# A two-layer hybrid decoder step on one core: old retention state in two loads, branch A's gate product taken apart, squares summed in column groups, output stored in pieces

## The reference, cut to what matters

```python
def _layer(x, pos, s_wkv, s_ret, s_shift, p):
    h = _rmsnorm(x, p['norm_mix_pre'])
    z = h @ p['w_in']
    ya, s_wkv, s_shift = _rwkv7_branch(za, s_wkv, s_shift, ...)     # branch A
    yb, s_ret = _retention_branch(zb, pos, s_ret, ...)              # branch B
    m = jax.nn.sigmoid(ga) * (ya @ p['w_out_a']) + jax.nn.sigmoid(gb) * (yb @ p['w_out_b'])
    x = x + _rmsnorm(m @ p['w_o'], p['norm_mix_post'])
    h = _rmsnorm(x, p['norm_ffn_pre'])
    f = (jax.nn.silu(h @ p['w_ffn_gate']) * (h @ p['w_ffn_up'])) @ p['w_ffn_down']
    x = x + _rmsnorm(f, p['norm_ffn_post'])

# end of branch A: y = (yn * gain + bias + bonus) * g, with yn = (y - mean) / sqrt(var + eps)
# in branch B, for the samples' old state S0:
    scores = jnp.einsum('bihd,bjhd->bhij', qc, kc) * d_in[None]
    cross = jnp.einsum('bihd,bhde->bihe', qc, S) * d_q[None, :, :, None]
```

## Time and profile before

| | us |
|---|---|
| median of 3 runs | 1365.44 (1364.4 to 1366.78) |
| the profiled execution, its own time | 1364.33 |
| span of its trace | 1362.5 |
| TensorE matmuls busy | 1306.5 (96%) |
| TensorE weight loads busy | 1231.8 (90%) |
| VectorE busy | 865.7 (64%) |
| ScalarE busy | 531.8 (39%) |
| GpSimd busy | 14.7 (1%) |

### The profile page before, as it was taken

The page is one execution under the profiler, slowest core; times in us unless marked ns, Lnnn a source line. Parts: engine busy times, 40 slices in busy tenths (PEclk is TensorE's granted clock), DMA queues, the critical chain, the costliest instruction groups (busy, mean ns, idle before and its releaser), DMA issues.

```text
span 1362.5 us, 27246 instructions
## 1 busy us (share of the span) xinstructions
PE 1306.5 (96%) x11896; PEld 1231.8 (90%) x11896; DVE 865.7 (64%) x1446; ACT 531.8 (39%) x803; POOL 14.7 (1%) x26
## 2 busy tenths in 40 slices
PE   6999999799998999999899999998999989999997
PEld 5899997789997999999888999977999979999996
DVE  4777757666776556653476876667666755656533
ACT  4552032344435333343446521232544354333433
POOL 0002000000000000000000020000000000000000
PEclk8999999899998999999989999998999989999999
DMA  5433223444443454544423322244444534444441
GB/s 201 139 111 126 53 94 118 158 148 152 145 142 124 155 154 153 155 143 151 150 72 115 129 83 71 76 170 156 141 139 132 170 109 125 152 154 142 155 153 56
DMA packets 50311, 179.48 MB, mean 132 GB/s; under 512 B 6161, under 2 KB 6673, under 8 KB 48785
## 3 DMA queue, kind: packets, MB, share of 16 engines
q1 hardware_dynamic: 41328, 150.49, 34.2%
q10 hardware_dynamic: 8864, 27.25, 6.1%
HBM read 166.57 MB, written 8.53 MB: 129 GB/s over the span
## 4 chain that ended last, share of the span: by engine, by line
PE 91%; DVE 4%; DMA 2%; ACT 2%; issue 1%; SPq 0%; ACTq 0%; DVEq 0%
PE dense L1104 53%; PE core L1104 37%; DMA ret<-ret_d 1%; DMA w_raw<-wts 1%; DVE w_lo L682 1%; ACT w_hi L427 1%; DVE x L721 1%; DVE y_out L719 0%; DVE y_a L959 0%; DVE y_a L960 0%; DVE ya_lo L701 0%; DVE y_a L958 0%; PE core L1255 0%; DVE ya_hi L700 0%; ACT L410 0%
## 5 line engine op out<-in xcount | busy, mean ns | idle before, releaser
L682 DVE TENSOR_TENSOR w_lo<-w_raw,w_hi 128x1024 fp32r<-128x1024 f32 x282 | 345.0, 1224 | 333.9 <-ACT w_hi L427 331.5
L427 ACT ACTIVATE w_hi<-w_raw 128x1024 fp32r<-128x1024 f32 x282 | 298.7, 1059 | 639.5 <-PE dense L1104 511.6
L1104 PE MATMUL dense<-h_hi,w_hi 128*128 128x320 f32 x1328 | 426.1, 321 | 19.3 <-DVE h_lo L741 10.1
L1104 PE MATMUL dense<-h_lo,w_hi 128*128 128x320 f32 x1328 | 414.4, 312 | 0.0
L1104 PE MATMUL dense<-h_hi,w_lo 128*128 128x320 f32 x1328 | 414.4, 312 | 0.0
L1104 PEld LDWEIGHTS dense<-h_hi,w_hi 128*128 128x128 f32 x1328 | 252.8, 190 | 30.8 <-issue 24.3
L1104 PEld LDWEIGHTS dense<-h_lo,w_hi 128*128 128x128 f32 x1328 | 253.4, 191 | 2.2
L1104 PEld LDWEIGHTS dense<-h_hi,w_lo 128*128 128x128 f32 x1328 | 253.1, 191 | 0.0
L1104 PE MATMUL core<-h_hi,w_hi 128*128 128x320 f32 x384 | 119.1, 310 | 0.0
L1104 PE MATMUL core<-h_lo,w_hi 128*128 128x320 f32 x384 | 119.1, 310 | 0.0
L1104 PE MATMUL core<-h_hi,w_lo 128*128 128x320 f32 x384 | 118.9, 310 | 0.0
(11 more groups left out here) (249 smaller groups left out, 1861.7 us busy)
## 6 DMA issues: line engine op xcount, KB each, us to landing
w_raw<-wts SPq DMA_DIRECT2D x282, 512.0 KB, 3.5
ret<-ret_d ACTq DMA_DIRECT2D x2, 2048.0 KB, 8.7
ret_t<-ret_t ACTq DMA_DIRECT2D x16, 256.0 KB, 4.1
ret_s<-ret_t ACTq DMA_DIRECT2D x16, 256.0 KB, 2.3
qk_rot<-qk_raw ACTq DMA_DIRECT2D x8, 320.0 KB, 6.4
dmask<-rconst ACTq DMA_DIRECT2D x2, 1152.0 KB, 5.8
s_st<-wkv_st ACTq DMA_DIRECT2D x2, 1024.0 KB, 5.4
wkv_s<-s_st ACTq DMA_DIRECT2D x2, 1024.0 KB, 3.9
```

Of the source, the lines that this page charges most:

```text
L427: act.activation(w_hi[n % RING][:, :], w_raw[n % RING][:, :], ACT.Copy).then_inc(hi_ready.sem, 1)
L682: dve.tensor_tensor(w_lo[r][:, :], w_raw[r][:, :], w_hi[r][:, :].bitcast(F32), ALU.subtract).then_inc(low_made.sem, 1)
L1104: return pe.matmul(out, lhsT, rhs, start=start, stop=stop)
```

## The change

There are four edits.

1. The first quarter of the old retention state, 128x1024, gets a buffer of its own (`ret0_first`, in room that branch A has left by then) and is loaded behind `rc_small`, after the samples' `u` step. The other three quarters are loaded where the whole was, and head pair 1 waits for them. `rc_small` moves by a quarter KB.
2. Branch A's end, (yn * gain + bias + bonus) * g, becomes yn * (gain * g) + (bias + bonus) * g. The two products with g are made early: four `gate_bonus` operations behind steps w 0, u 0, as1 and as2, and four on `y_a` behind the squares in TAIL. `finish_ya` is left with four operations a chunk in place of five, and chunks 2 and 3 are finished after the copies to `o_b`.
3. The FFN's squares are summed with 32 columns of ones: four chunks go to the four column strips of one PSUM bank, twice. ScalarE copies the result to `acc`, and one matmul with a selecting matrix (`pick`) adds the four strips, now behind the fourth weight tile. It takes the place of an unused constant.
4. The output is stored in five pieces, each when its group of x is done, and the last layer's `x_root(3)` with its squares and sums is left out.

```diff
+BONUS_AFTER = [("w", 0), ("u", 0), ("as1", SAMPLE), ("as2", SAMPLE)]
-        ret0 = at("ret0", 20, 4096)
-        rc_small = at("rc_small", 3.75, NRC - R_DQ)
+        ret0 = [at("ret0_first", 0, 1024), at("ret0_rest", 20, 3072)]
+        rc_small = at("rc_small", 4, NRC - R_DQ)
...
-            sp.wait_ge(*x_done(DEPTH - 1, len(X_GROUPS)))
-            sp.dma_start(y_t, x[:, :]).then_inc(y_stored, 16)
-            sp.wait_ge(y_stored, 16)
+            for i, (lo, hi) in enumerate(X_GROUPS):
+                sp.wait_ge(*x_done(DEPTH - 1, i + 1))
+                sp.dma_start(y_t[:, lo * T:hi * T], x[:, lo * T:hi * T]).then_inc(y_stored, 16)
+            sp.wait_ge(y_stored, 16 * len(X_GROUPS))
...
                 act.dma_start(rc_small[:, :], rconst[:, R_DQ:NRC]).then_inc(rcs_loaded.sem, 16)
+                act.dma_start(ret0[0][:, :], ret_d[layer][:, 0:1024]).then_inc(ret0_first.sem, 16)
...
-                act.dma_start(ret0[:, :], ret_d[layer]).then_inc(ret0_loaded.sem, 16)
+                act.dma_start(ret0[1][:, :], ret_d[layer][:, 1024:4096]).then_inc(ret0_rest.sem, 16)
...
                 high(T_GU + EARLY - 1)
+                act.wait_ge(*x_partial(layer, 1))
+                act.activation(acc[:, :], core[0][:, 0:T], ACT.Copy).then_inc(x_parted.sem, 1)
                 x_root(2)
...
-                for c in range(KT):
-                    act.wait_ge(*x_done(layer, X_GROUP_OF[c] + 1))
-                    act.activation(ch(sq8, c), ch(x, c), ACT.Square).then_inc(x_squared.sem, 1)
-                x_root(3)
+                if layer + 1 < DEPTH:
+                    for c in range(KT):
+                        act.wait_ge(*x_done(layer, X_GROUP_OF[c] + 1))
+                        act.activation(ch(sq8, c), ch(x, c), ACT.Square).then_inc(x_squared.sem, 1)
+                    x_root(3)
...
+                def gate_bonus(i):
+
+                    dve.scalar_tensor_tensor(ch(bonus, i), ch(bonus, i), vec("gna_b", i), ch(g_a, i), ALU.add, ALU.mult).then_inc(bonus_gated.sem, 1)
...
+                    if step in BONUS_AFTER:
+                        gate_bonus(BONUS_AFTER.index(step))
...
                         dve.tensor_tensor(ch(sq_a, i), ch(y_a, i), ch(y_a, i), ALU.mult).then_inc(cent_a.sem, 1)
+                        dve.wait_ge(*cent_a(layer, i + 1))
+                        dve.scalar_tensor_tensor(ch(y_a, i), ch(y_a, i), vec("gna_g", i), ch(g_a, i), ALU.mult, ALU.mult).then_inc(y_gated.sem, 1)
...
-                def finish_ya():
+                def finish_ya(i):
...
-                        link(dve.scalar_tensor_tensor(y, y, vec("gna_g", i), ch(sq_a, i), ALU.mult, ALU.mult))
-                        link(dve.scalar_tensor_tensor(y, y, vec("gna_b", i), ch(bonus, i), ALU.add, ALU.add))
-                        link(dve.tensor_tensor(y, y, ch(g_a, i), ALU.mult))
-                        split(ch(ya_hi, i), ch(ya_lo, i), y).then_inc(ya_ready.sem, 1)
-                    dve.wait_ge(*ya_ready(layer, HP))
+                    y = ch(y_a, i)
+                    link(dve.tensor_tensor(y, y, ch(sq_a, i), ALU.mult))
+                    link(dve.tensor_tensor(y, y, ch(bonus, i), ALU.add))
+                    split(ch(ya_hi, i), ch(ya_lo, i), y).then_inc(ya_ready.sem, 1)
...
                     if hp == 0:
-                        finish_ya()
+                        for i in (0, 1):
+                            finish_ya(i)
...
                         make_qexp(hp + 1)
+                    if hp == 0:
+                        for i in (2, 3):
+                            finish_ya(i)
+                        dve.wait_ge(*ya_ready(layer, HP))
...
-                    if hp == 0:
-                        pe.wait_ge(*ret0_loaded(layer, 1))
+                    if hp < 2:
+                        pe.wait_ge(*(ret0_rest if hp else ret0_first)(layer, 1))
...
                         if q == 0 and i in (1, 2):
-                            for c in range(4 * i - 4, 4 * i):
-                                x_sum(2, c)
+                            for j in range(4):
+                                c = 4 * i - 4 + j
+                                pe.wait_ge(*x_squared(layer, KT + c + 1))
+                                ins = mm(core[0][32 * j:32 * j + 32, 0:T], ones[:, 0:32], ch(sq8, c), i == 1, i == 2)
+                            if i == 2:
+                                ins.then_inc(x_partial.sem, 1)
+                        if q == 0 and i == 3:
+                            pe.wait_ge(*x_parted(layer, 1))
+                            mm(core[0][:, 0:T], pick, acc[:, :]).then_inc(x_summed.sem, 1)
...
                 norm_sum(2)
-                for c in range(KT):
-                    x_sum(3, c)
+                if layer + 1 < DEPTH:
+                    for c in range(KT):
+                        x_sum(3, c)
```

More of the change, by code:

```diff
@@ L38 @@
 NPV = sum(w for _, w in PV.values())
-F_ID, F_BLK, F_PERM, F_ONES, F_I2, F_BD, F_SEQ, F_EPS, NFX = 0, 128, 256, 384, 512, 576, 578, 586, 589
+F_ID, F_BLK, F_PICK, F_ONES, F_I2, F_BD, F_SEQ, F_EPS, NFX = 0, 128, 256, 384, 512, 576, 578, 586, 589
 M_X1T, M_X1, M_STRT, M_STR, M_INC, M_LT, M_RST = 0, 64, 128, 256, 384, 512, 832
@@ L86 @@
 N_ROUNDS = 5 * NST + HP * 14 + 5
-ACT_STEPS, DVE_STEPS = 13, 240
+ACT_STEPS, DVE_STEPS = 13, 236
 def program(nc, x_t, wts, pvec, lora, shift0, fixed, rmask, trig, rconst, wkv_st, ret_d, ret_t,
@@ L206, in program @@
         dense_evac_v, = many(60, "dense_evac_v")
-        (lora_loaded, shift_loaded, mask_loaded, trig_loaded, s0st_loaded, ret0_loaded,
+        (lora_loaded, shift_loaded, mask_loaded, trig_loaded, s0st_loaded, ret0_first, ret0_rest,
          shift_stored, wkvs_stored, wkvp_stored, retp_stored) = many(
             1, "lora_loaded", "shift_loaded", "mask_loaded", "trig_loaded", "s0st_loaded",
-            "ret0_loaded", "shift_stored", "wkvs_stored", "wkvp_stored", "retp_stored", unit=16)
+            "ret0_first", "ret0_rest", "shift_stored", "wkvs_stored", "wkvp_stored", "retp_stored", unit=16)
         rcs_loaded, dmask_loaded = many(1, "rcs_loaded", "dmask_loaded", unit=16)
@@ L218, in program @@
         x_summed, x_rooted = many(2, "x_summed", "x_rooted")
+        x_partial, x_parted = many(1, "x_partial", "x_parted")
         h_scaled, = many(KT, "h_scaled")
@@ L230, in program @@
         kk_root, root_a = many(1, "kk_root", "root_a")
-        kk_made, = many(HP, "kk_made")
+        kk_made, bonus_gated, y_gated = many(HP, "kk_made", "bonus_gated", "y_gated")
         k_ready, b_ready = many(1, "k_ready", "b_ready")
@@ L326, in bc @@
             return ap.unsqueeze(axis).broadcast_to(shape[:axis] + [n] + shape[axis:])
-        ident, blk, perm, ones = (fx[:, o:o + 128] for o in (F_ID, F_BLK, F_PERM, F_ONES))
+        ident, blk, pick, ones = (fx[:, o:o + 128] for o in (F_ID, F_BLK, F_PICK, F_ONES))
         i2 = fx[:, F_I2:F_I2 + C]
@@ L666, in _ @@
                 norm_root(2)
-                for c in range(KT):
-                    act.wait_ge(*x_done(layer, X_GROUP_OF[c] + 1))
-                    act.activation(ch(sq8, c), ch(x, c), ACT.Square).then_inc(x_squared.sem, 1)
-                x_root(3)
-                assert steps[0] == ACT_STEPS, steps
+                if layer + 1 < DEPTH:
[3 more added lines that the diff above has]
+                    x_root(3)
+                    assert steps[0] == ACT_STEPS, steps
             for s in (shift_stored, wkvs_stored, wkvp_stored, retp_stored, *rets_stored):
@@ L951, in _ @@
                 dve.wait_ge(*sts_clear(layer, 1))
-                def finish_ya():
-                    dve.wait_ge(*root_a(layer, 1))
-                    for i in range(HP):
-                        y = ch(y_a, i)
-                        link(dve.scalar_tensor_tensor(y, y, vec("gna_g", i), ch(sq_a, i), ALU.mult, ALU.mult))
-                        link(dve.scalar_tensor_tensor(y, y, vec("gna_b", i), ch(bonus, i), ALU.add, ALU.add))
-                        link(dve.tensor_tensor(y, y, ch(g_a, i), ALU.mult))
-                        split(ch(ya_hi, i), ch(ya_lo, i), y).then_inc(ya_ready.sem, 1)
-                    dve.wait_ge(*ya_ready(layer, HP))
+                def finish_ya(i):
+                    if i == 0:
+                        dve.wait_ge(*root_a(layer, 1))
+                        dve.wait_ge(*bonus_gated(layer, HP))
+                        dve.wait_ge(*y_gated(layer, HP))
+                    y = ch(y_a, i)
+                    link(dve.tensor_tensor(y, y, ch(sq_a, i), ALU.mult))
+                    link(dve.tensor_tensor(y, y, ch(bonus, i), ALU.add))
+                    split(ch(ya_hi, i), ch(ya_lo, i), y).then_inc(ya_ready.sem, 1)
                 def finish_yb(hp):
@@ L1389, in _ @@
                     pe.wait_ge(*qexp_ready(layer, hp + 1))
-                    if hp == 0:
-                        pe.wait_ge(*ret0_loaded(layer, 1))
+                    if hp < 2:
+                        pe.wait_ge(*(ret0_rest if hp else ret0_first)(layer, 1))
```

(6 more changed lines are left out.)

## The result

The changed kernel takes **1343.72 us** (median of 4 runs, 1343.19 to 1344.25). The kernel before, run beside it, takes 1365.76 us (4 runs, 1364.4 to 1366.78). The ratio is 0.9839, with a 95% interval of 0.9822 to 0.9856: 22.0 us faster, where 22.1 were forecast. Of the later runs of the kernel before, 21 in one session had a median of 1364.74, so the gain is nearer to 21 us. In two of the kernels of the experiments one run lay far out (3263 us, one of 4, and 2545 us, one of 11), which hardly moves their medians. The profiled execution after took 1344.25 us with a span of 1342.5, 20.0 less than before's.

A forecast was written before the change was run, and what follows sets the result against it. TensorE, 91% of the chain that ended last, was taken as the bound. Gains of 15.6 + 4.3 + 2.2 = 22.1 us took the profiled 1364.33 to 1342.2, so the median forecast was 1343.3 us, range 1339 to 1350.

The forecast's parts named there:

- The first wait: Head pair 0: TensorE's idle 4.91 and 4.08 us for the old state become 1.9 us a layer, ended by `q_exp`.
- The second wait: Head pair 0: TensorE's wait for VectorE's copies into `o_b`, 2.5 us a layer, goes, with 2.0 us to spare.
- The rival that it stays in part: VectorE, `w_hi` or a weight tile late in head pair 0; gives back 8.4 us at most, 1345 to 1351.7; chance 0.12.
- The clock: Head pair 0: one half-speed stretch of 1.6 us in the two layers, taking 17.2 us of gain to 15.6 (14.0 to 17.2).
- The squares: FFN sums on column strips: 0.81 us a round of four, 4.3 us gained for two layers (3.9 to 5.4).
- The root's way: FFN: later root hidden by 1.0 us; rival, 1 to 2 us longer, TensorE waits for the bank, 1345 to 1348; chance 0.07.
- The end: Output store: last 320 KB piece lands in 2.3 us where one store took 4.5; gain 2.2 us (1.5 to 2.5).
- The sum: Whole kernel: 15.6 + 4.3 + 2.2 = 22.1 us gained, median forecast 1343.3 us.

The follow-up runs named there:

- early `q_exp`: Changed kernel with VectorE's first `q_exp` of a layer and the clearing of `sts` moved behind the last `s` step of TAIL: 1336.86 us.
- filled: Changed kernel with eight unused 128x128 matmuls put ahead of TensorE's wait for `q_exp` in each layer: 1343.85 us.
- the order alone: Changed kernel with the old formula for branch A's end, no early products, but still two chunks ahead of the copies and two behind: 1344.2 us.
- the one strip: Changed kernel with all eight sums of squares, still 32 columns wide, one after the other on the same column strip: 1351.04 us.
- the formula alone: Changed kernel with the split products kept, but all four chunks finished ahead of the copies: 1343.78 us.
- the kernel with the wait filled and the store moved: Changed kernel with eight unused matmuls in the `q_exp` wait and ScalarE's `ret_p` store issued behind the last branch B roots: 1341.17 us.

## Why the prediction came out

**The first wait: right.** 1.94 us remained in each layer, ended by `q_exp`, as worked out.

**The second wait: right.** It fell in both layers, with more to spare than the 2.0 us worked out (3.9), since the slow tiles hold TensorE back and a chunk takes 1.81 and not 1.88. The rival that it stays in part didn't come, and the two experiments on order and formula show why it was less likely than its 0.12: either half of the edit would have been enough, to within 0.6 us. The state's update had 2.0 us to spare; with the old formula it became a wait of 0.6.

**The clock: the step that was mis-sized.** I took one slow stretch of 1.6 us in the two layers. It came in both: 8.77 - 7.04 = 1.73 and 8.70 - 7.04 = 1.66, 3.4 in all. The traces give 7.35 and 6.39 us for head pair 0 (from branch A's last variance sums to the end of the 16-entry block: 36.71 before and 29.36 after in layer 0), 13.7 together where I had 15.6. With the 3.4 added back this is 17.1, and the sum at full clock was 17.2. The range for this step, 14.0 to 17.2, was a little too narrow, because it counted a slow stretch at 1.6 and left nothing for the clock's other wobbles. With the early `q_exp` the two tiles take 7.24, so 1.5 of each 1.7 was the clock, and it comes with the wait: in the five kernels that kept this wait it followed in nine layers of ten, in the three without it (filled or gone) in none of six.

**The squares: right, at the low end.** Four sums took 0.67 and the tile behind them 0.19 more, 0.86 where I held 0.81. For one layer this is 4.3 - 2 x 0.86 - 0.54 = 2.04, 4.1 for two, against 4.3; alone the edit gave 3.8, just under the bound of 3.9 but with an interval of 2.6 to 5.7. By "TensorEngine Tiling (Array Packing)" of the Trainium skill, Tiling Modes, a change of the mode drains TensorE. The 0.19 may be that; the trace shows the time and not its reason. From trace to trace the FFNs' start gained only 1.50 and 1.77, because in the changed kernel's profile the clock was at half for longer there. The root's way became no wait: no row of TensorE's waits names it.

**The end: right.** From the same tile near the end of the FFN to the span's end it is 43.63 before and 41.41 after, 2.22. The 320 KB landed in 2.2 us, where the estimate from "DMA: Bandwidth & Descriptors" of the Trainium skill, Anatomy of one DMA, was 2.75; the measurement decides. That section of the Trainium skill fits DMAs that GpSimd issues, while SyncE issues this one; the prediction left that out. But my reason was half of it: I had the omitted work beside the store and so worth nothing, while without the omission the root would have ended last and 0.6 be lost.

**The sum.** Trace to trace it is 13.7 + 3.3 + 2.2 = 19.2, and 0.8 from other places: 1.1 won between the layers and 0.6 in layer 1's branch A, 0.7 lost ahead of head pair 0 in layer 0 and 0.3 behind head pair 3. That is 20.0, where I had 22.1. The forecast of the median met all the same, since the profiled execution before lay 1.4 under the median of its runs and the one after 0.5 above. So part of the hit, about 2 us, is luck.

## What to carry to other kernels

When one wait goes, ask what the next operation in its way is: here `q_exp`, one 0.42 us operation behind two others in VectorE's queue, was worth 7 us, a third of the whole change, and nearly half of that was the slow clock behind the wait. Count a wait of TensorE with the stretch behind it, and expect that stretch behind most such waits (here behind nine of ten), not behind all. And where time is won ahead of transfers, look at which issues they now meet: an issue that blocks its engine can take the gain back half a stage later.

## What was unexpected of the hardware

- The granted clock fell to half behind the wait of 1.94 us for `q_exp`, in both layers in the profiles of the changed kernel, the early quarter alone, the order alone and the one strip, and in layer 1 of the formula alone. It did so after the wait, with TensorE busy again. With the wait filled or gone it did not. But in layer 0 of the formula alone it stayed at 1.00 behind the same 1.94 us, and so it did behind 1.9 us of waiting for `s_ga` in layer 1 of the kernel with the wait filled and the store moved, and behind the 1.2 us of that wait in layer 0 of the changed kernel. The length of one wait does not settle it, and what does was not found.
- The issue of a store of 256 KB occupied ScalarE's queue for 0.47 us in one run and 1.78 in another, of two such stores 0.83 and 2.39. The longer ones came with stores of `ret_s` that landed in 3.7 to 3.9 and not 2.2 us. But in layer 0 of the last of these kernels they landed in 3.7 and the issue took 0.84. The next weight tile is not what differs: its issue came 2.3 us behind that of the first `ret_s` in the quick cases and in the slow ones, and in all of them the DMA engines stood idle when the stores began. The cause was not found.
- Four sums of 320 columns on four column strips take 0.67 us, one of 128 output partitions alone 0.54, four on one strip 3.15 - 0.88 = 2.27.
